# Held-back projection blocks behind the RWKV recurrence: moved from ahead of the norm's factor to behind it

## What is computed

```python
y = _rwkv7_scan(r_h, w_h, k_h, v_h, kh, a_h)
mean = jnp.mean(y, axis=-1, keepdims=True)
var = jnp.mean((y - mean) ** 2, axis=-1, keepdims=True)
y = (y - mean) * lax.rsqrt(var + RW_GN_EPS)
y = y * gn_gain + gn_bias
y = y + jnp.sum(r_h * k_h * r_k, axis=-1, keepdims=True) * v_h
return y.reshape(bsz, t_len, BRANCH_W) * gate
```

## Time and profile before

| | |
|---|---|
| three timed runs | 3274.01, 3276.19, 3278.99 us |
| median | 3276.19 us |
| the profiled execution's own time | 3268.32 us |
| its span, first to last instruction | 3266.6 us |
| PE busy | 3161.2 us, 97% of the span |
| granted TensorE clock, mean | 0.990 |
| layer 1's output norm, PE | 690.96 to about 736.7 us |

### The profile page before, as it was taken

The page is one execution under the profiler, slowest core; times in us unless marked ns, Lnnn a source line. Parts: engine busy times, 40 slices in busy tenths (PEclk is TensorE's granted clock), DMA queues, the critical chain, the costliest instruction groups (busy, mean ns, idle before and its releaser), DMA issues. The chain is left out here.

```text
span 3266.6 us, 68685 instructions
## 1 busy us (share of the span) xinstructions
PE 3161.2 (97%) x29414; PEld 2930.6 (90%) x29414; DVE 1883.7 (58%) x2867; ACT 1356.9 (42%) x2303; POOL 685.6 (21%) x538
## 2 busy tenths in 40 slices
PE   9999999999999999999999999999999999999997
PEld 8999999987788999999999999999877778879986
DVE  7884156435767435886078832464467674368832
ACT  4444252324554325444254442523245553354441
POOL 1003335110012441002300043342100125500042
PEclk9999999999999999999999999999999999999999
DMA  3333222002111332333233332220121213333331
GB/s 106 103 104 102 61 71 59 4 22 64 44 49 40 88 91 71 112 97 107 59 104 104 104 88 62 69 49 4 32 61 46 53 39 94 87 104 102 105 94 49
DMA packets 378443, 237.30 MB, mean 73 GB/s; under 512 B 16766, under 2 KB 376460, under 8 KB 378140
## 3 DMA queue, kind: packets, MB, share of 16 engines
q1 hardware_dynamic: 378140, 232.91, 24.8%
HBM read 230.50 MB, written 2.10 MB: 71 GB/s over the span
## 5 line engine op out<-in xcount | busy, mean ns | idle before, releaser
L671 POOL TENSOR_TENSOR W_low<-W,W_high 128x512 fp32r<-128x512 f32 (+1 forms) x176 | 215.4, 1248 | 1267.7 <-ACT W_high L782 1267.7
L155 PE MATMUL PS<-u_high,dW_high 128*128 128x264 f32 (+1 forms) x1344 | 411.9, 306 | 14.5 <-POOL dW_low L2200 8.4
L157 PE MATMUL PS<-u_high,dW_low 128*128 128x264 f32 (+1 forms) x1344 | 384.8, 286 | 0.0
L156 PE MATMUL PS<-u_low,dW_high 128*128 128x264 f32 (+1 forms) x1344 | 384.6, 286 | 0.0
L782 ACT ACTIVATE W_high<-W 128x1024 fp32r<-128x1024 f32 (+1 forms) x236 | 241.2, 1027 | 317.5 <-PE PS L157 190.0
L156 PE MATMUL PS<-hidden_low,W_high 128*128 128x264 f32 (+1 forms) x1232 | 369.6, 300 | 0.0
L155 PE MATMUL PS<-u_high,W_high 128*128 128x264 f32 (+1 forms) x1152 | 361.7, 314 | 5.1 <-POOL W_low L2200 2.4
L157 PE MATMUL PS<-u_high,W_low 128*128 128x264 f32 (+1 forms) x1152 | 355.8, 309 | 0.0
L728 PE MATMUL PS<-u_high,W_high 128*128 128x264 f32 (+1 forms) x1152 | 330.8, 287 | 5.1 <-ACT s L782 2.1
L729 PE MATMUL PS<-u_low,W_high 128*128 128x264 f32 (+1 forms) x1152 | 326.9, 284 | 0.0
L730 PE MATMUL PS<-u_high,W_low 128*128 128x264 f32 (+1 forms) x1152 | 326.9, 284 | 0.0
(11 more groups left out here) (453 smaller groups left out, 8404.5 us busy)
## 6 DMA issues: line engine op xcount, KB each, us to landing
W<-in_ffn_w_in SPq DMA_DIRECT2D x160, 512.0 KB, 5.2
dW<-in_w_in SPq DMA_DIRECT2D x172, 256.0 KB, 2.9
W<-in_ffn_w_out SPq DMA_DIRECT2D x64, 512.0 KB, 4.1
W<-in_w_in SPq DMA_DIRECT2D x80, 256.0 KB, 3.0
W<-in_ffn_w_out SPq DMA_DIRECT2D x32, 384.0 KB, 3.4
W<-in_w_branch SPq DMA_DIRECT2D x48, 256.0 KB, 2.8
W<-in_ffn_w_in SPq DMA_DIRECT2D x32, 256.0 KB, 4.9
W<-in_w_out SPq DMA_DIRECT2D x32, 256.0 KB, 2.8
```

Source lines behind the costliest of these rows:

```text
L155: nc.tensor.matmul(dst, wh, xh, start=first, stop=False)
L156: nc.tensor.matmul(dst, wh, xl, start=False, stop=False)
L157: return nc.tensor.matmul(dst, wl, xh, start=False, stop=final)
L671: ins = g.tensor_tensor(dst, src, high.bitcast(F32), ALU.subtract)
```

## The change

It moves calls on PE's list and alters no other engine's code. The group of blocks between `bonus(0)` and `squares(3)` goes; so do those behind `bonus(2)` and behind `gates(2)`. Of the eight groups five are left, of 3, 2, 3, 3 and 13 blocks; the new tuple has two more numbers that no line reads. The 24 blocks and all steps of the norm are the same.

```diff
-                    GIVEN = (3, 3, 4, 3, 3, 3, 3, 2)
+                    GIVEN = (3, 2, 3, 3, 3, 3)
...
                     bonus(0)
-                    tiles.blocks(pe, GIVEN[0])
                     squares(3)
                     bonus(1)
-                    tiles.blocks(pe, GIVEN[1])
+                    tiles.blocks(pe, GIVEN[0])
                     pe.wait_ge(S("var_rsqrt"), 1)
                     spread_out(0)
                     pe.wait_ge(S("bonus_out"), 1)
                     bonus(2)
-                    tiles.blocks(pe, GIVEN[2])
                     pe.wait_ge(S("bonus_out"), 2)
                     bonus(3)
...
                     spread_out(1)
-                    tiles.blocks(pe, GIVEN[3])
+                    tiles.blocks(pe, GIVEN[1])
                     pe.wait_ge(S("bonus_out"), 4)
                     gates(1)
                     pe.wait_ge(S("scaled"), 2)
                     spread_out(2)
-                    tiles.blocks(pe, GIVEN[4])
+                    tiles.blocks(pe, GIVEN[2])
                     pe.wait_ge(S("gated"), 1)
                     gates(2)
-                    tiles.blocks(pe, GIVEN[5])
                     pe.wait_ge(S("scaled"), 3)
                     spread_out(3)
-                    tiles.blocks(pe, GIVEN[6])
+                    tiles.blocks(pe, GIVEN[3])
                     pe.wait_ge(S("gated"), 2)
                     gates(3)
                     tiles.blocks(pe, KD * tiles.tiles - tiles.given)
```

## The result

| kernel | median us (runs) | lowest to highest | profiled run: us, span, clock |
|---|---|---|---|
| before | 3271.91 (12) | 3265.32 to 3279.09 | 3268.32, 3266.6, 0.990 |
| after | 3279.59 (12) | 3270.64 to 3286.89 | 3273.73, 3272.0, 0.988 |

The ratio is 1.0023, with an interval of [1.0013, 1.0033]: the change makes the kernel slower by 0.23%. The difference is 7.7 us by the medians, 6.7 us by the means (3278.71 against 3272.06). The time was forecast as 3277.6 us and lies 2.0 us above that. But the forecast started from a median of three runs, 3276.19, and nine further runs of before brought it down by 4.3 us. So the difference was forecast as +1.4 us and came out near +7.

A forecast was written before the change was run, and what follows sets the result against it. It took PE, busy 97% of the span, and its clock as the bound. Two layers at -0.15 us plus 1.7 us for one extra low stretch gave +1.4 us, hence 3277.6 us with the carried 7.87; range 3270 to 3284.

The forecast's parts named there:

- The order's own terms: Per layer, what reordering PE's list costs apart from the clock: -0.3 us for groups, +0.15 us new wait, sum -0.15 us.
- The wait ahead of `gates(0)`: PE waits there for DVE's product of `bonus(2)`, since `bonus(3)` follows at once: 0.15 us, bounds 0 and 0.4.
- The 0.79 us for ACT's copy: Tile boundaries: one bare wait for the PSUM bank, now inside the last 13 blocks; net 0, 0.2 us either way.
- three groups fewer save 0.3 us: Eight block groups become five, saving three late starts of 0.10 us per layer: -0.3 us, bounds 0 and -0.6.
- The clock: Behind layer 1's squares the clock stays low at 707.0 for 3.4 us more, costing 1.7 us; bounds 0 and -3.4.
- That sign: Layer 1's second low stretch, behind the squares, should last past 707.0, to about 710.4 us.
- so I count the extra stretch once in the two layers: One extra low stretch, in layer 1 only, since layer 2 begins shifted: +1.7 us in all; chance 0.42.
- the rival "faster": The second low stretch behind the squares is gone in both layers: -7.1 us, 3269.1 us; chance 0.06.
- The 7.87 us between profile and median: Offset from the profiled run of before, 3268.32, to the timed median, 3276.19, added to the forecast unchanged.
- 0.86 for "within 0.2%": Summed chance of one, none or two extra low stretches, all within 6.6 us, not distinguishable from no change.
- The rivals around the clock: Behind the squares, no extra low stretch (-0.3 us, 3275.9, chance 0.28) or one in both layers (+3.1, 3279.3, 0.16).
- The rival "slower": `gates(0)` and `spread_out(3)` each wait one DVE round of 2.06 us per layer: +9.3 us, 3285.5; chance 0.08.

The follow-up runs named there:

- e8: The changed kernel run once more, in a later series beside before: median 3278.18 us, ratio 1.0021 to before.
- e2: Against before, only the first half of the change: squares(3) and bonus(1) ahead of the blocks, later groups as before; 3274.02 us, ratio 1.0016.
- e10: The changed order with 12 more projection matmuls (1.45 us) per layer, so the norm begins later; 3274.52 us, ratio 1.0015 to before.
- the control: The order of before written with plain numbers in place of the tuple of group sizes, same instruction order; 3269.60 us, ratio 1.0003 to before.
- e12: The changed order with two lines swapped, bonus(0) behind squares(3) instead of in front; 3267.89 us, ratio 0.9995 to before.
- e11: Against before, all forty squares in a row, then both bonus sums, then blocks, later groups as before; 3270.50 us, ratio 1.0004.
- e4: Against before, two blocks between each two of the four sums of squares, taken from three later groups; 3271.87 us, ratio 1.0000.

## Why the prediction was right, and where it was wrong

**What bounds the kernel: right.** PE's clock and not the norm's factor. The wait that the change could shorten had no length, and the factor 3.1 us earlier by the program's own progress (4.2 in time from the start of the program) bought nothing.

**The order's own terms: right, and too small to see.** The wait ahead of `gates(0)` was put at 0.15 us with bounds 0 and 0.4: `bonus(2)` and `bonus(3)` take 710.81 to 712.77, the product is there at 712.72, and no wait shows. The 0.79 us for ACT's copy stand inside the last 13 blocks, once. That three groups fewer save 0.3 us can be neither seen nor excluded: the work column does not resolve it.

**The clock: the right term, sized too small.** In layer 1 the stretch behind the squares lasts 3.4 us longer, as forecast; it began 1.1 us earlier and ended at 709.3 and not at 710.4. That sign came true in part by luck: of four executions with the change at this place, two have 10.2 us there in layer 1 (after, e8) and two 6.8 (e2, e10). `squares(3)` took 1.79 us at the lower level, where 2.0 was put. `spread_out(0)` comes straight from a block, at 709.57; that is 13.17 us behind the first square in place of 13.77, so 0.6 us earlier by the program's own progress and not 2: the blocks that no longer stood ahead of it were paid for by the lower clock.

The step that failed is "so I count the extra stretch once in the two layers": a term of +1.7 us. Against the later runs of before the lost time rose by 7.2 to 8 us, which is as much as four or five such stretches. Two things were missing in that step. It took the one profile's low stretch of 6.8 us for what the order of before does, where the control shows 3.4 us for the same instructions, and none at all in its layer 2; and it looked for the extra time only behind the squares, where three executions of either order show 5.7 us more at the lower level, 2.8 us lost. Where the rest is lost stays open.

The reason for the term was half right. The prediction expected the clock to stay low because only 2.0 us of wide matmuls would stand behind the last square by 707.0, `squares(3)` having moved into the low stretch. e12 confirms that the second burst is what matters. But against the rival "faster" it argued that all forty squares stand closer together, "which is what it fell behind", and in e11 and e12, where they stand closest, no cost can be seen.

**The rule that was weighed.** The Trainium skill ("TensorE: Matmul & The Clock Gate", Part 1) ties the gate to how busy the engine is. By it a mere change of order is worth the -0.3 us of the groups; measured are +6.7. With squares of 48 columns the order is indeed worth nothing (0.6 ± 0.9 us); with two columns PE was busy 10.20 of 10.20 us and the clock stood at 0.51. With the same section's statement that the gate's check runs freely the traces agree: one order of instructions gave a stretch of 6.8 us and one of 3.4 in two executions.

**The base and the chances.** The 7.87 us between profile and median, carried over from three runs, were 3.6 by twelve. That error of 4.3 us and the missing 5 to 6 us of clock nearly cancel: the predicted time is close for a wrong reason, by luck. 0.86 for "within 0.2%", 6.6 us, was too sure: measured are 6.7 us by the means and 7.7 by the medians. The rivals around the clock allowed one or two extra stretches in the whole program, though nothing in the rows held them to the two places looked at; with four or more the difference passes 6.6 us. The rival "slower" is not what happened, though its +9.3 us is the nearest of all in size: its waits of 2.06 us show nowhere.

## What to carry to other kernels

Where PE is busy 97% of the time, moving instructions so that a result is ready earlier is worth nothing unless a wait for it shows, and it can cost clock: look at what stands around matmuls that stream a few columns. A second burst of them soon after the first cost 7 us here, and swapping two lines, so that all of them stood together with only wide matmuls behind, gave them back; the order of before, with 18 block matmuls between the bursts, does not pay them either. Judge such an edit by span times granted clock and by the rest, each over many runs: one profile's low stretches are a draw.

## What the runs showed of the hardware

- PE's granted clock can fall while PE is busy throughout: in after it fell near 699.1, behind matmuls of two columns, with PE busy 3.40 of 3.40 us, and stayed at 0.51 for 10.20 us, all busy. Behind matmuls of 48 columns that take nearly as long (3.60 us for thirty against 3.31) it stayed at 1.00 in six norms of six; behind those of two columns it fell in 19 of 20, e4 with its blocks in between left out.
- The scatter between runs of one kernel is the clock's too: in after's twelve runs, from 3270.64 to 3286.89 us, time and mean granted clock have a correlation of -0.93.
- At the lower level a block's matmul starts every 0.22 us in place of 0.12, and the squares, whose weights are loaded anew each time, slow down too, though they stream two columns: ten took 1.79 us (702.05 to 703.84) in place of 1.09.
- Work added on PE did not show in the time here: 24 matmuls more (2.9 us) gave -0.4 ± 1.4 us, with 2.7 us less lost; why is open.
